# Two groups of gate and up tiles in block 1 computed as seven block products a pair, and the weight sums for it

## The reference

```python
for l in range(2):                                  # block 1
    hn = rms_norm(h, norm_mix_g[l])
    q, k, v, xr, gate = split(hn @ w_in[l])
    h = h + concat([norm(diff_attention(q, k, v)), norm(rg_lru(xr, gate))]) @ w_out[l]
    hn = rms_norm(h, norm_ffn_g[l])
    g, u = jnp.split(hn @ w_gu[l], [D_FF], axis=-1) # D_FF = 2816 = 22 tiles of 128
    h = h + (jax.nn.silu(g) * u) @ w_down[l]
for l in range(2):                                  # block 2, 512 tokens
    x = norm(a * x + mixers(x))                     # convolution, top-k and band attention
    x = norm(a * x + cross_attention(x, mem))
    x = norm(a * x + relu(x @ w1[l]) ** 2 @ w2[l])  # 4096 = 32 tiles
```

## Time and profile before

| | us |
|---|---|
| median of 3 runs | 2840.27 (2839.78 to 2840.6) |
| the profiled execution | 2839.67 |
| its span | 2837.8 |
| TensorE busy | 2757.3 (97%) |
| VectorE busy | 1760.2 (62%) |
| ScalarE busy | 1308.1 (46%) |
| GpSimd busy | 484.6 (17%) |

### The profile page before, as it was taken

The page is one execution under the profiler, slowest core; times in us unless marked ns, Lnnn a source line. Parts: engine busy times, 40 slices in busy tenths (PEclk is TensorE's granted clock), DMA queues, the critical chain, the costliest instruction groups (busy, mean ns, idle before and its releaser), DMA issues.

```text
span 2837.8 us, 41613 instructions
## 1 busy us (share of the span) xinstructions
PE 2757.3 (97%) x16644; PEld 2379.3 (84%) x16648; DVE 1760.2 (62%) x2709; ACT 1308.1 (46%) x2225; POOL 484.6 (17%) x401
## 2 busy tenths in 40 slices
PE   9999999999989999999999999999999999999997
PEld 8878999999877788887668888998776688889996
DVE  6786545454777745454875558555758764686555
ACT  5674322234675432223564546443445645464433
POOL 2221121001222022000333120000313331200003
PEclk9999999999999999999999999999999999999999
DMA  4112787422112588432213222444321232234442
GB/s 153 45 46 68 211 195 197 117 92 82 53 46 67 181 221 217 120 94 96 64 61 125 98 67 90 149 137 131 109 82 56 74 121 89 75 93 145 147 129 81
DMA packets 115712, 313.74 MB, mean 111 GB/s; under 512 B 12992, under 2 KB 14656, under 8 KB 115520
## 3 DMA queue, kind: packets, MB, share of 16 engines
q1 hardware_dynamic: 84672, 256.16, 27.9%
q0 software_dynamic: 13824, 25.17, 5.6%
q10 hardware_dynamic: 17024, 29.75, 3.1%
HBM read 308.93 MB, written 52.43 MB: 127 GB/s over the span
## 4 chain that ended last, share of the span: by engine, by line
PE 87%; DVE 7%; ACT 4%; issue 2%; POOL 0%; DMA 0%; ACTq 0%; DVEq 0%; SPq 0%
PE psum L644 21%; PE psum L650 21%; PE psum L647 21%; PE psum L1266 3%; PE psum L1269 3%; PE psum L1271 3%; PE psum L716 2%; PE psum L739 1%; PE psum L743 1%; PE psum L741 1%; PE psum L977 1%; PE psum L1005 1%; PE psum L1150 1%; PE psum L1162 1%; PE psum L994 1%
## 5 line engine op out<-in xcount | busy, mean ns | idle before, releaser
L1299 ACT ACTIVATE weights_hi_lo<-weights_float 128x1024 fp32r<-128x1024 f32 (+2 forms) x482 | 502.2, 1044 | 556.0 <-PE psum L650 412.2
L1917 DVE TENSOR_TENSOR weights_hi_lo<-weights_float,weights_hi_lo 128x1024 fp32r<-128x1024 f32 (+2 forms) x468 | 584.7, 1250 | 259.1 <-ACT weights_hi_lo L1299 257.8
L644 PE MATMUL psum<-act_hi_lo,weights_hi_lo 128*128 128x264 f32 (+2 forms) x2160 | 628.4, 337 | 3.7 <-ACT temp L1403 2.8
L647 PE MATMUL psum<-act_hi_lo,weights_hi_lo 128*128 128x264 f32 (+2 forms) x2160 | 602.9, 325 | 1.9 <-DVE weights_hi_lo L1917 1.9
L650 PE MATMUL psum<-act_hi_lo,weights_hi_lo 128*128 128x264 f32 (+2 forms) x2160 | 603.1, 325 | 0.0
L644 PE MATMUL psum<-hidden_hi_lo,weights_hi_lo 128*128 128x512 f32 (+2 forms) x1584 | 519.4, 357 | 3.6 <-DVE x_residual L2171 1.4
L650 PE MATMUL psum<-hidden_hi_lo,weights_hi_lo 128*128 128x512 f32 (+2 forms) x1584 | 510.9, 352 | 1.4 <-DVE hidden_hi_lo L2181 1.4
L647 PE MATMUL psum<-hidden_hi_lo,weights_hi_lo 128*128 128x512 f32 (+2 forms) x1584 | 510.8, 352 | 1.3 <-DVE weights_hi_lo L1917 1.3
L644 PEld LDWEIGHTS psum<-act_hi_lo,weights_hi_lo 128*128 128x128 f32 x2160 | 367.9, 189 | 53.1 <-issue 17.7
L647 PEld LDWEIGHTS psum<-act_hi_lo,weights_hi_lo 128*128 128x128 f32 x2160 | 367.1, 189 | 33.0 <-issue 2.6
L650 PEld LDWEIGHTS psum<-act_hi_lo,weights_hi_lo 128*128 128x128 f32 x2160 | 366.6, 189 | 33.2
(11 more groups left out here) (324 smaller groups left out, 4266.8 us busy)
## 6 DMA issues: line engine op xcount, KB each, us to landing
weights_float<-in_w_gu SPq DMA_DIRECT2D x88, 512.0 KB, 3.4
weights_float<-in_w_ff SPq DMA_DIRECT2D x80, 512.0 KB, 3.6
weights_float<-in_w_in SPq DMA_DIRECT2D x70, 512.0 KB, 3.2
weight_sums<-in_w_ff ACTq DMA_DIRECT2D x24, 1024.0 KB, 5.5
weights_float<-weight_sums SPq DMA_DIRECT2D x96, 256.0 KB, 2.8
weights_float<-in_w_ff SPq DMA_DIRECT2D x72, 256.0 KB, 2.9
weights_float<-in_w_down SPq DMA_DIRECT2D x32, 448.0 KB, 3.4
weight_sums<-in_w_ff POOLq DMA_DIRECT2D x48, 256.0 KB, 5.9
```

The costliest lines, as they stand in the source:

```text
L644: e.matmul(slot[:, place:place + c1 - c0], w_hi[:, col], x_hi[:, c0:c1], start=first, stop=False)
L647: e.matmul(slot[:, place:place + c1 - c0], w_lo[:, col], x_hi[:, c0:c1], start=False, stop=False)
L1299: e.activation(K.parts(n)[0][:, 0:cols], K.staged(n)[:, 0:cols], ACT.Copy).then_inc(*K.did("hi", n))
L1917: e.tensor_tensor(lo[:, 0:cols], K.staged(n)[:, 0:cols], hi[:, 0:cols].bitcast(F32), ALU.subtract).then_inc(*K.did(name, n))
```

## The change

The second and third group of each layer (tiles 8 to 14 and 15 to 21) are computed as block products: tile f of the gate and tile f of the up part are a pair, so a group has 7 pairs of 7 products, each of 4 chunks x 3 matmuls over half the width (264 or 256 columns). The pieces of these groups hold two products' weights each (25 pieces, the last half full). The products need the normed input scaled by its gain and root (`scaled1`), split again in high and low parts, and 4 sums of its blocks for 4 chunks (`sums1`, `sums1_low`); this is done in the tiles and downs of group 0. The pairs' halves are put together on ScalarE and VectorE (`scalar_forms1`, `vector_forms1`), and slots in PSUM are given by tables (`DOWN_SLOTS`, `FORM_SIDE1`).

The weight sums of block 1 are 2 groups x 7 pairs x 4 sums a layer. ScalarE copies at steps 10 to 52 of the attention (8 copies of 1792 KB a layer), GpSimd adds 28 in steps 34 to 61 and 28 after the attention. The sums of block 2 go to its mixers (12 copies a layer at steps 18 to 62, 40 adds at steps 28 to 106) and cross attention (8 adds). A memset of the meta rows on GpSimd is done again for layer 1.

```diff
+COPY_STEPS = {10 + 6 * (4 * g + s): (f0, s) for g, f0 in enumerate((8, 15)) for s in range(4)}
+COPY_STEPS2 = {18 + 4 * (4 * g + s): (f0, s) for g, f0 in enumerate(FF2_FIRST[1:]) for s in range(4)}
+SUM_STEPS1 = {34 + n: n for n in range(4 * FORM_PAIRS1)}
+SUM_STEPS2 = {28 + 2 * n: n for n in range(40)}
+SUM_STEPSX = {2 + 2 * n: 40 + n for n in range(8)}
...
+def tensor_forms1(e, w, K, B, l, f0):
...
+    for p in range(FORM_PAIRS1):
+        side = (p + FORM_SIDE1[f0]) % 2
+        banks = [4 * side + b for b in range(4)]
+        for j in range(7):
...
+            if j == 2:
+                w.wait_ge(*done("first1", l, f0, p))
+            if j == 5:
+                w.wait_ge(*done("third1", l, f0, p))
+            if j == 6:
+                w.wait_ge(*done("inner1", l, f0, p))
...
+            for k in range(DC // 2):
...
+                e.matmul(K.bank[b][:, 0:half], w_hi[:, col], x_hi, start=not adds and k == 0, stop=False,
+                         skip_group_check=adds)
+                w.wait_ge(*K.low(n))
+                e.matmul(K.bank[b][:, 0:half], w_lo[:, col], x_hi, start=False, stop=False, skip_group_check=adds)
+                w.wait_ge(*there[1])
+                mm = e.matmul(K.bank[b][:, 0:half], w_hi[:, col], x_lo, start=False,
+                              stop=k == DC // 2 - 1, skip_group_check=adds)
...
+def scalar_forms1(e, w, K, l, f0):
...
+        if j == 0:
+            e.activation(first[:, half], X, ACT.Copy, scale=-1.0).then_inc(*did("first1", l, f0, p))
+        if j == 1:
+            e.activation(third[:, half], V, ACT.Copy).then_inc(*did("third1", l, f0, p))
+        if m % 2 == 1 or m == FORMS1 - 1:
+            split_hi(e, w, K, PIECE["form1", l, f0, m // 2] + 3)
+        if j == 5:
+            w.wait_ge(*done("upper1_other", l, f0, p))
+            e.activation(b, a, ACT.Tanh, scale=0.5).then_inc(*did("silu_tanh", l, f))
+        if j == 0 and p > 0:
+            hidden_high(f - 1)
...
+            e.scalar_tensor_tensor(K.scaled1[f][:, 0:width], K.m["x"][:, f, T1 - width:T1], K.par(l, "ffn_g", f),
+                                   K.root[:, 0:width], ALU.mult, ALU.mult).then_inc(*did("scaled_x", l, f))
...
+                for k in {0: (0, 1), 2: (2, 3, 4), 4: (5, 6, 7)}.get(n, ()):
+                    hi, lo = K.act_chunk(k, width)
+                    w.wait_ge(*done("act1_hi", l, k))
+                    e.tensor_tensor(lo, K.scaled1[k][:, 0:width], hi.bitcast(F32), ALU.subtract).then_inc(*did("act1_lo", l, k))
+                if n in (1, 3):
+                    sums1(e, w, K, l, 2 + n // 2)
+                if n in (0, 1, 3, 5):
+                    sums1_low(e, w, K, l, (0, 1, 3, 5).index(n))
...
+def vector_forms1(e, w, K, l, f0):
...
+        if j == 3:
+            e.tensor_tensor(outer, first, Z, ALU.add).then_inc(*did("outer1", l, f0, p))
+        if j == 4:
+            e.tensor_tensor(inner, third, W, ALU.add).then_inc(*did("inner1", l, f0, p))
+        if j == 5:
+            e.tensor_tensor(a[:, half], outer, V, ALU.add).then_inc(*did("upper1", l, f0, p))
+            e.tensor_tensor(a[:, other], a[:, half], inner, ALU.subtract).then_inc(*did("upper1_other", l, f0, p))
+        if j == 6:
+            w.wait_ge(*done("silu_tanh", l, f))
+            e.scalar_tensor_tensor(a, b, 1.0, a, ALU.add, ALU.mult).then_inc(*did("silu", l, f))
+            e.scalar_tensor_tensor(a[:, half], X, 0.5, a[:, half], ALU.mult, ALU.mult).then_inc(*did("first_hidden1", l, f0, p))
+            e.tensor_tensor(b[:, other], W, outer, ALU.subtract).then_inc(*did("lower1", l, f0, p))
+            e.scalar_tensor_tensor(a[:, other], b[:, other], 0.5, a[:, other], ALU.mult, ALU.mult).then_inc(
+                *did("hidden", l, f))
+        if m % 2 == 1 or m == FORMS1 - 1:
+            split_lo(e, w, K, PIECE["form1", l, f0, m // 2] + 3)
...
+def pool_sum1(e, w, K, l, n):
...
+    if step == 0:
+        w.wait_ge(*done(f"copied1_{SUM_GROUPS1.index((l, f0))}", 3))
+    if p == 0 and s == 1:
+        w.wait_ge(*done("weight_sum0", "1", l, f0, FORM_PAIRS1 - 1))
+    if p == 0 and s == 3:
+        w.wait_ge(*done("weight_sum2", "1", l, f0, FORM_PAIRS1 - 1))
+        w.wait_ge(*done("weight_sum1", "1", l, f0, FORM_PAIRS1 - 1))
+    src = K.block1(l, f0, p, 1, 0) if s in (0, 2) else K.weight_sum1(l, f0, p, 0 if s == 1 else 1)
+    e.dma_start(K.weight_sum1(l, f0, p, s), src, accum_op=ALU.add, max_dma_last_dim=4 * FORM).then_inc(
+        *did(f"weight_sum{s}", "1", l, f0, p, by=16))
```

More of the change, by code:

```diff
@@ L287 @@
 HALF = T2 // 2
+HALF1 = T1 // 2
+SUMS1 = 2 * 4 * DC // 2 * HALF1
 FORM = DC // 2 * P
@@ L935, in tensor_ffn1 @@
     for f0, f1 in FF_GROUPS:
-        for f in range(f0, f1):
+        if f0 > 0:
+            tensor_forms1(e, w, K, B, l, f0)
+        for f in range(f0, f1 if f0 == 0 else f0):
             g = (PIECE["w_gu", l, f], RING["w_gu", l, f, 0], ("gated", l, f))
@@ L1501, in scalar_ffn1 @@
             e.dma_start(K.pos_i[:, 0:T2].bitcast(I32), K.t["positions"]).then_inc(*did("landed_positions", by=16))
-        for f in range(f0, f1):
+        if f0 > 0:
+            scalar_forms1(e, w, K, l, f0)
+        for f in range(f0, f1 if f0 == 0 else f0):
             a, b = (tile[:, 0:width] for tile in K.hid_work[f % 2])
@@ L2240, in vector_ffn1, with sums1 @@
                           lambda n: ("added", "w_down", l, f0, n), width)
+def sums1(e, w, K, l, k):
+    did, done = K.did, K.done
+    width = T1 if l + 1 < DEPTH else T2
+    half = width // 2
+    (a1, a2), (b1, b2) = ((K.scaled1[chunk][:, 0:half], K.scaled1[chunk][:, half:width]) for chunk in (k, k + DC // 2))
+    s1, s2, s3, s4 = (tile[:, 0:half] for tile in K.float1[k % 2])
+    w.wait_ge(*done("scaled_x", l, DC - 1))
+    if k >= 2:
+        w.wait_ge(*done("sum1_lo", l, 3, k - 2))
+    e.tensor_tensor(s3, a1, a2, ALU.subtract).then_inc(*did("sum1", l, 2, k))
+    e.tensor_tensor(s1, a2, b2, ALU.subtract).then_inc(*did("sum1", l, 0, k))
+    w.wait_ge(*done("sum1", l, 2, k))
+    e.tensor_tensor(s2, s3, b2, ALU.add).then_inc(*did("sum1", l, 1, k))
+    w.wait_ge(*done("sum1", l, 1, k))
+    e.tensor_tensor(s4, b1, s2, ALU.subtract).then_inc(*did("sum1", l, 3, k))
@@ L2882, in pool_program @@
         pool_attention(e, w, K, l)
-        for group in SUM_GROUPS:
-            if group[0] == l:
-                pool_sums(e, w, K, *group)
+        for n in range(len(SUM_STEPS1), 2 * 4 * FORM_PAIRS1):
+            pool_sum1(e, w, K, l, n)
+        if l + 1 < DEPTH:
+            w.wait_ge(*K.done("product", PIECE["form1", l, FF_GROUPS[-1][0], FORMS1 // 2]))
+            e.memset(K.v[:, 4, :], 0.0).then_inc(*K.did("meta_zero", l + 1))
         if l + 1 < DEPTH:
```

247 lines of the change are left out of this document (203 added, 44 removed).

## The result

The changed kernel takes 2863.12 us (median of 4 runs, 2861.93 to 2863.59) against 2840.43 before: ratio 1.0081, 95% interval 1.0065 to 1.0097. It is 22.7 us slower, and outside the range 2806 to 2838. The likeliest forecast failed; the rival given 0.08, GpSimd's queue in the attention, came true.

What follows compares the result with a forecast made beforehand. TensorE was taken to bound the kernel, busy for 2757.3 of 2837.8 us. The terms summed as 2839.67 - 29.1 + 1 + 2 + 6 + 2 = 2821.6, say 2822 us (chance 0.66), with 2806 to 2838 as the range for 8 in 10.

Steps and rivals of the forecast that it cites:

- GpSimd's queue in the attention: Rival, chance 0.08: blocked issues delay scalings, VectorE's combination, then TensorE's output product; near 2870 us if half reaches TensorE.
- The products: Groups two and three: 588 narrower matmuls a group take 72.6 us in layer 0, 71.2 in layer 1; -29.1 us in all.
- The rule of the Trainium skill: Weight loads priced by columns, overlapping products only on other row groups; the products would win nothing, sum 2851 us.
- Seams: Four form groups with their seams: fuller VectorE delays TensorE, and the first down needs the last pair's low half; +1 us (0 to 3).
- the second split: Splitting the scaled normed input, with its sums, in group 0's tiles and downs fits beside VectorE's other work; 0 us.
- ScalarE's copies: Attention: 16 copies of 1792 KB on ScalarE, up to 0.8 us each, which TensorE sometimes waits for; +2 us (0 to 12.8).
- GpSimd's sums in the attention: 28 a layer in steps 34 to 61: most issues should not block, a few delay scalings; +6 us (0 to 111).
- The adds behind: The other 28 sums, after the attention, end at 360 us, before the third group, which began at 537.07; 0 us.
- Block 2's mixers: 24 copies on ScalarE and 96 issues on GpSimd in the mixers, at every second step, mostly hidden; +2 us (0 to 91).
- All is hidden: Rival, chance 0.17: attention and mixers absorb the issues wholly, leaving the products' gain and the seams; 2812 us.
- the chain of VectorE: Rival, chance 0.08: in the form groups, with VectorE at 85%, a late split moves every pair; 2840 to 2849 us.
- The prediction's first reading: Both groups of a layer take the same time with or without weight sums beside them, so TensorE's columns count.

Runs made afterwards that it cites:

- half rows: Changed kernel, but the 28 adds in each attention add only the first 64 of 128 rows, the other half left out; 2824.7 us.
- spread: Changed kernel, but the 28 adds in each attention are spread over steps 32 to 78 instead of one a step; 2823.95 us.
- mixers later: Changed kernel, but block 2's adds begin at step 36 of the mixers instead of 28, 36 there and 12 in the cross attention; 2855.72 us.
- copies early: Changed kernel, but layer 1's 8 copies are issued in layer 0's form pairs, its adds staying in the attention; 2861.0 us.
- all behind: Changed kernel, but all block 1's adds come behind the attention, and block 2's copies and adds return to block 1's feed-forward part; 2850.73 us.

## Why the prediction was wrong

1. **The products, -29.1.** Right: -30.8. A product took 72.05 / 588 = 122.5 ns in layer 0 (taken: 123.5) and 120.7 in layer 1 (121.1). The rule of the Trainium skill weighed there (TensorE: Matmul & The Clock Gate, "LDWEIGHTS") gave an estimate of 126 us for a group of layer 1; the run shows 70.9.
2. **Seams, +1, and the second split, 0.** TensorE shows no gap in the forms of layer 0, 0.2 us in those of layer 1, none in the downs. VectorE is at 77% in a form group where I had 85%.
3. **ScalarE's copies, +2.** 0 by themselves (the attentions at +1.9 and -1.6 with the copies and no adds). But they are not free beside the adds, whose landing they delay: about 12.7 of the second attention's 20.4 us went with them.
4. **GpSimd's sums in the attention, +6.** The step that failed: +41.3 (20.9 and 20.4). Its upper end was worked out as 3/8 of 56 issues at 5.3 us, 111 us of standing. That is what came: 51.4 us in ten waits in the first attention and 56.7 in ten in the second, 108 us. That it fits so closely is in part luck, since without the copies ten waits took 37.4 us. I argued it away with "an issue comes every 2.9 us, and three in flight cover 8.7 us against a landing of 6.3: most should not block". The mistake is in comparing with one landing: the earlier trace rows show three issues and then a wait of 7.1 us, the next burst 9.9 us after the first, so the queue took one add in 3.3 us there (behind the changed kernel's first attention 28 adds were issued from 296.8 to 379.1, one in 3.0). At one in 2.9 there was no room left, least of all beside copies. The 2.9 itself came out of a stretch, 690 to 925, that runs past the end of the steps near 880; steps 34 to 61 took 3.0 us each in the kernel before, so it was right by luck. Against the 108 us of standing TensorE lost 41 us, about a third of it in longer matmuls, most of them at the lower granted clock after the gaps (6.7 of 20.9 us in the first attention, 7.1 of 20.4 in the second). Not all of the 41 is the queue's: with 3.1 and 3.9 us of standing (half rows) the attentions still took 3.4 and 4.0 us more.
5. **The adds behind, 0.** In time for the third group, as said. But layer 1's tiles of group 0 took 3.4 us more: VectorE waits 1.7 us for the load of the positions, with splits behind it, and TensorE 3.0 for a split. That load, while GpSimd issues adds:

```profile
temp<-in_positions ACTq DMA_DIRECT2D x1, 256.0 KB, 4.5
```

It was 2.7 us before. In every kernel in which it landed in 4.3 to 4.7 us (changed, spread, mixers later, copies early, half rows) these tiles took 82.2 to 83.2; in all with 2.6 to 2.9 us they took 78.8 to 80.5. That it is the cause was not tried by itself.

6. **Block 2's mixers, +2.** +9.6, cross attention within. Most of it is not the count of issues: an add placed two steps ahead of the copy that it needs made 6.6 of it. Where the other 3.0 us went is open.

"All is hidden" would have been right for the forms alone; the chain of VectorE was no bound. The rival of GpSimd's queue named the chain (issue, scaling, combination, output product) and 2870, and stood in the text with nearly the right size (55 us in the attentions, measured 41). It got 0.08 because an estimate from a mean spacing stood against a count of blocked issues. The prediction's first reading was off too: "taking block 2's sums out of this place wins nothing" held for the plain tiles; beside forms these sums have a price ("all behind": 78.1 us for a group of 72.1 beside block 2's adds alone).

## What to carry to other kernels

A DMA that GpSimd issues stands in GpSimd's program: when its queue was full here (51.4 us in ten waits), everything behind it in that program waited. Compare the rate of issues with the rate that the queue has shown in a long run of them (here one add of 256 KB in 3.0 to 3.3 us), not with the time of one landing, and if a trace counts the blocked ones, believe the count. Before background transfers go beside a stage, add up the bandwidth of the stage as it will be after the change: a faster form that reads more weights leaves less room (here 12.8 MB in 72 us in place of 7.3 in 82).

## What was not expected of the hardware

- The price of a queue's standing is far from proportional: in the first attention 20.3 us of it came with 3.4 us lost (spread) and 51.4 with 20.9; in the second 26.7 with 3.1 (spread), 37.4 with 7.7 (copies early) and 56.7 with 20.4.
- Adds of half the rows, with half the bytes and packets, took the standing from 51.4 to 3.1 us with as many issues. An add of 128 KB still took 5.2 and 3.9 us to land (5.7 and 5.2 for 256 KB, all in the second attention), so the landing time alone doesn't tell when the queue is full.
- Sums and copies beside the forms keep the DMA engines busy to a share of 0.96 at 257 GB/s and stretch a group by 11.4 us (6.1 beside adds alone, at 0.94), where 0.73 beside plain tiles cost nothing.
